# One decoder step on one core: both parts of a head's values in one stationary tile, and four waits of TensorE moved

## The reference

```python
n = rms_norm(x, g_mix)                       # the first norm
q, k, v, hc, bc, cc = split(n @ w_in)        # 16 heads of 64; 1024 conv channels
q, k = rms_norm(q, q_norm), rms_norm(k, k_norm)
attn = dilated_attention(q, k, v, rel_bias)  # softmax(q k / 8 + bias) @ v
conv = bc * short_conv(cc * hc)
h = x + concat[rms_norm(attn), rms_norm(conv)] @ w_out
h = h + (silu(n2 @ w_gate) * (n2 @ w_up)) @ w_down     # n2 = rms_norm(h)
h = h + sigmoid(rms_norm(h) @ w_ple_gate) * (p @ w_ple_proj)
```

## Time and profile before

| | |
|---|---|
| median of 3 runs | 2536.05 us (2533.64 to 2537.11) |
| the profiled execution's own time | 2535.68 us |
| its span, first to last instruction | 2534.1 us |
| PE busy | 2481.5 us, 98% |
| DVE, ACT, POOL busy | 69%, 37%, 10% |
| mean granted clock of TensorE | 0.992 of 2.4 GHz |

### The profile page before, as it was taken

The page is one execution under the profiler, slowest core; times in us unless marked ns, Lnnn a source line. Parts: engine busy times, 40 slices in busy tenths (PEclk is TensorE's granted clock), DMA queues, the critical chain, the costliest instruction groups (busy, mean ns, idle before and its releaser), DMA issues.

```text
span 2534.1 us, 51880 instructions
## 1 busy us (share of the span) xinstructions
PE 2481.5 (98%) x20462; PEld 2467.8 (97%) x20462; DVE 1753.1 (69%) x2194; ACT 933.4 (37%) x1201; POOL 252.9 (10%) x281
## 2 busy tenths in 40 slices
PE   5999999999989999999999999999999999999998
PEld 5999999999989999999999999999999999999998
DVE  5576777777786899898888889888533322356433
ACT  4333333333432444444444444444322222233331
POOL 1111110111111000000000000000000000143000
PEclk8999999999999999999999999999999999999999
DMA  5343333333333423333433333343655443233331
GB/s 187 121 135 116 124 108 110 106 125 109 118 119 114 162 93 137 118 133 117 150 127 138 133 116 133 116 143 129 222 191 180 161 142 118 78 91 103 112 112 67
DMA packets 99741, 324.00 MB, mean 128 GB/s; under 512 B 18258, under 2 KB 18514, under 8 KB 99168
## 3 DMA queue, kind: packets, MB, share of 16 engines
q1 hardware_dynamic: 72144, 250.25, 30.2%
q0 software_dynamic: 26672, 70.69, 8.1%
q10 hardware_dynamic: 864, 2.24, 0.2%
HBM read 286.80 MB, written 40.65 MB: 129 GB/s over the span
## 4 chain that ended last, share of the span: by engine, by line
PE 93%; DVE 3%; DMA 2%; issue 1%; ACT 1%; POOL 0%; ACTq 0%; DVEq 0%; SPq 0%
PE acc L560 18%; PE acc L564 18%; PE acc L562 18%; PE acc L765 11%; PE acc L766 11%; PE acc L764 11%; DMA wraw<-in_w_down 1%; PE aux L571 1%; PE aux L609 1%; PE aux L653 1%; DVE wlo L1252 1%; PE aux L583 0%; PE aux L582 0%; PE aux L581 0%; PE aux L622 0%
## 5 line engine op out<-in xcount | busy, mean ns | idle before, releaser
L1252 DVE TENSOR_TENSOR wlo<-wraw,whi 128x1024 fp32r<-128x1024 f32 (+1 forms) x276 | 333.3, 1208 | 396.2 <-ACT whi L904 395.5
L904 ACT ACTIVATE whi<-wraw 128x1024 fp32r<-128x1024 f32 (+1 forms) x276 | 285.5, 1035 | 705.5 <-PE acc L564 651.7
L764 PE MATMUL acc<-xb_hi,whi 128*128 128x260 f32 x1228 | 347.7, 283 | 4.4 <-DVE xb_lo_t L1643 4.4
L765 PE MATMUL acc<-xa_lo,whi 128*128 128x260 f32 x1228 | 348.4, 284 | 0.0
L766 PE MATMUL acc<-xa_hi,wlo 128*128 128x260 f32 x1228 | 348.3, 284 | 0.0
L766 PE MATMUL acc<-xb_hi,wlo 128*128 128x260 f32 x1228 | 347.4, 283 | 0.0
L764 PE MATMUL acc<-xa_hi,whi 128*128 128x260 f32 x1228 | 346.8, 282 | 0.0
L560 PE MATMUL acc<-slots_a,whi 128*128 128x260 f32 x1536 | 313.3, 285 | 0.0
L564 PE MATMUL acc<-slots_a,wlo 128*128 128x260 f32 x1536 | 309.4, 283 | 0.0
L562 PE MATMUL acc<-slots_a,whi 128*128 128x260 f32 x1536 | 309.4, 283 | 0.0
L560 PE MATMUL acc<-slots_b,whi 128*128 128x260 f32 x1408 | 284.7, 284 | 4.8 <-ACT hid L1194 3.2
(11 more groups left out here) (290 smaller groups left out, 5087.0 us busy)
## 6 DMA issues: line engine op xcount, KB each, us to landing
wraw<-in_w_in SPq DMA_DIRECT2D x96, 512.0 KB, 3.6
blocks<-in_w_gate SPq DMA_DIRECT2D x88, 512.0 KB, 6.0
blocks<-in_w_up SPq DMA_DIRECT2D x88, 512.0 KB, 5.9
wraw<-in_w_down SPq DMA_DIRECT2D x48, 448.0 KB, 3.4
wraw<-in_w_out SPq DMA_DIRECT2D x32, 512.0 KB, 3.5
wraw<-in_w_ple_gate SPq DMA_DIRECT2D x32, 512.0 KB, 3.6
slots_b<-f_dram SPq DMA_DIRECT2D x28, 520.0 KB, 4.6
f_dram<-sig_t POOLq DMA_DIRECT2D x22, 520.0 KB, 3.2
```

Of the source, the lines that this page charges most:

```text
L764: mm(to, w_h, hi, start=p == 0, stop=False)
L765: mm(to, w_h, lo, start=False, stop=False)
L904: on(whi[:, u % HILO, 0:width], wraw[:, u % RAW, 0:width], ACT.Copy).then_inc(s_whi, 1)
L1252: V.tensor_tensor(wlo[:, u % HILO, 0:width], wraw[:, u % RAW, 0:width], whi[:, u % HILO, 0:width].bitcast(F32), ALU.subtract).then_inc(s_w ...
```

## The change

Six edits. **Values:** one tile `v_both` holds, for each head e, the high part in that head's 64 columns and the low part of the same values in the other 64. One pass with the high probabilities and one with the low ones then give the high sums in the head's own 64 rows and the low sums in the other 64. ACT copies the low rows across to `o_low`, DVE adds them. ACT writes the high part in two copies, DVE the low part in two subtractions. **First norm:** the squares come in four groups behind g = 0 to 3, the sum over partitions behind unit 5, its spreading behind unit 6; q too is copied out unscaled, and k, q and v are scaled at g = 6. **x:** the piece 0 goes first on SP, ahead of the first weights; SP takes the even pieces and ACT the odd ones. **Last attention:** it stands behind units 3 to 14 of the conv half, with what follows it (the last operand at i = 13, the attention norm at i = 15). **Down:** the first two units of chunk 0 go to four spare banks. **Hidden tiles** of chunk 1 are loaded one to a unit from m = 5, the last three in chunk 1, which waits for its two parts apart.

```diff
-X_SQUARES = (range(0, 5), range(5, 10), range(10, KT))
+X_SQUARES = (range(0, 4), range(4, 8), range(8, 12), range(12, KT))
...
+    def first_down(m):
+        return (spare, spare_low, acc_of(0), acc_of(1))[m]
...
@@ SP
-                    load_x(1)
-                    load_x(3)
+                    load_x(2)
...
-                    load_x(5)
-                    load_x(7)
+                    load_x(4)
+                    load_x(6)
+        load_x(0)
         pair(FIRST, 0, first=True)
...
+            if m >= 5:
+                load_hidden(1, m - 5)
...
@@ PE
-                    done = products(aux[:, BANK_O, (q0 + skip) * P:(q0 + 2) * P], vhi[:, kb, :], vlo[:, kb, :],
-                                    pthi[:, kb, skip:2, :], ptlo[:, kb, skip:2, :], kb == 0,
-                                    kb == max(q0, 1))
+                    out, values = aux[:, BANK_O, (q0 + skip) * P:(q0 + 2) * P], v_both[:, kb, pair_of // 2, :]
+                    mm(out, values, pthi[:, kb, skip:2, :], start=kb == 0, stop=False)
+                    done = mm(out, values, ptlo[:, kb, skip:2, :], start=False, stop=kb == max(q0, 1))
...
-                if a is None and g == 2:
+                if a is None and g == 5:
                     pe.wait_ge(s_bias, 1)
                     pe.wait_ge(s_xadd, KT - 1)
...
-            if i == 3:
-                pe.wait_ge(s_read, T_CONV + 3)
-            if 2 <= i <= PAIR_UNITS + 1:
-                attention(KA - 1, i - 2, final=True)
+            if 3 <= i <= PAIR_UNITS + 2:
+                attention(KA - 1, i - 3, final=True)
...
+        pe.wait_ge(s_nroot, N_FFN)
         for b in range(4):
-            if b < 2:
-                pe.wait_ge(s_ev, 6 * PAIRS - 2 * (1 - b))
-            if b == 0:
+            if b >= 2:
                 pe.wait_ge(s_cp, 2 * PAIRS)
-            else:
-                pe.wait_ge(s_read, T_D + b - 1)
+                pe.wait_ge(s_ev, 6 * PAIRS)
...
@@ ACT
+            if g in (5, 9):
+                e = (g - 5) // 4
+                act.wait_ge(s_pv, 4 * a + 2 * (e + 1))
+                on(o_low[e * HD:(e + 1) * HD, :], aux[(1 - e) * HD:(2 - e) * HD, BANK_O, :], ACT.Copy).then_inc(s_olow, 1)
...
-        for g in range(0, PIECES, 2):
+        for g in range(1, PIECES, 2):
...
@@ DVE
-                dve.wait_ge(s_pv, 4 * a + 2 * (e + 1))
-                V.tensor_copy(hid[e * HD:(e + 1) * HD, a, 0:SEQ], aux[e * HD:(e + 1) * HD, BANK_O, :]).then_inc(s_o, 1)
+                rows = slice(e * HD, (e + 1) * HD)
+                dve.wait_ge(s_olow, 2 * a + e + 1)
+                V.tensor_tensor(hid[rows, a, 0:SEQ], aux[rows, BANK_O, :], o_low[rows, :], ALU.add).then_inc(s_o, 1)
```

## The result

The changed kernel takes **2514.19 us** (median of 4 runs, 2513.75 to 2514.97) against 2536.08 us before (4 runs beside it): ratio 0.9915, 95% interval 0.9902 to 0.9927. It is faster by 21.9 us, not by 30. The profiled execution took 2514.97 us, with a span of 2513.4.

A forecast was written before the change was run, and what follows sets the result against it. PE, busy 2481.5 of 2534.1 us, was taken to bound the kernel. Terms 14.5 + 10.2 + 2.4 + 3.0 = 30.1 us, taken from 2535.7, gave 2505.6 us; the range was 2495 to 2517.

The forecast's parts named there:

- rival (b): Value products: removed matmuls were not the bound, PE waits for the probabilities instead; 2514 to 2525 us, chance 0.14.
- First norm, 14.5: First turn: earlier PE start and sums without a wait, less a new wait for v's copy; 14.5 us, bounds 12.9 to 19.5.
- fall of the clock: First turn, behind PE's wait for the copy of v: a stretch at half clock, costing 2.0 us.
- Value products, 10.2: Pair loop and last attention: 96 fewer matmuls on PE save 10.2 us, bounds 9.5 and 11.0.
- The 0.5 of the last attention: Value products there: 12 of the removed matmuls, worth 1.4 us, counted as 0.5 because DVE is late.
- The cover of ACT's copy: Value products: two units of PE work hide ACT's copy of low rows, cost nothing; uncovered, 9.6 us.
- Last attention, 2.4: Start of conv half: later attention saves 2.4 us of PE's waiting, half clock stays; bounds 0 and 5.0.
- the wait for unit 1: Start of conv half: PE's unit 3 waits some 4.3 us for DVE's reading of unit 1.
- Start of down, 3.0: Start of down: spare banks and hidden-tile order remove waits and half clock; 3.0 us, bounds 0.5 and 6.1.
- PE's waits for `hid`: Start of down: PE's waits for ACT's copies would remain at 1 to 3 us in all.

The follow-up runs named there:

- experiment 5: Changed kernel with POOL's load of cached values one unit later and DVE's copy of v ahead of four additions of squares: 2502.52 us.
- experiment 7: Kernel before with only the value products changed (two passes instead of three, ACT's copy of the low rows, DVE's addition): 2529.42 us.
- experiment 2: Changed kernel with the last attention back behind units 2 to 13 of the conv half, POOL's queue as before: 2511.11 us.

## Why the prediction held, and where it missed

Sign and range held; the gain was 21.9 us where I had 30.1. The time lies just past the band of my own forecast (2498 to 2514), in the band that I had given to rival (b), but (b) is not why: the removed matmuls paid in the seven turns, and the loss stands in the last attention. That the range held with such a loss in it is owed to its width. By its own steps:

- **First norm, 14.5: right** (14.0), and by its steps: PE's start, the wait for the copy of v with a fall of the clock, sums without a wait. Small misses cancel: the wait was 0.5 us longer, and units 4 and 5 took 54.88 - 41.74 = 13.1 us where two units take 11.7, so that the fall of the clock cost 1.4 and not 2.0. (Two figures of the prediction are a little off: unit 2 of the kernel before ended at 49.39 - 15.03 = 34.4 and not 34.2, and 2505.6 less 2.0 is 2503.6.) How much of the 14.0 the earlier start gives by itself was not tried apart. That the additions ahead of the copy are what PE's wait for v comes from is shown by experiment 5, where only their order changes.
- **Value products, 10.2: mechanism right, size off** (8.5 - 0.6 = 7.9 by experiment 7). The seven turns of the changed kernel give 8.6 / 84 = 0.102 us a matmul; I had read 0.115 off two steps of one timeline. The 0.5 of the last attention was a small loss, by rival (b). The cover of ACT's copy held.
- **Last attention, 2.4: the step that failed.** It came out as a loss, outside its bounds of 0 and 5.0, though the wait for unit 1 came as forecast (4.35 for 4.3). The step followed PE and DVE and did not name POOL, which carries the residual tiles and the load of cached values for this stage in one queue. The one line left behind there cost 2514.2 - 2506.7 = 7.5 us, of which 220.4 - 213.3 = 7.1 in this stretch: 5.6 of waiting and some 2.6 of the 5.3 us at half clock, less 1.2 of new short waits, in sum 7.0 by these rows. With it moved, the stretch wins 3.4, near the 2.9 that I had, but by luck: the shift is worth 4.1 by experiment 2 and not 2.4, and the products lose some 0.6 where I had a gain of 0.5.
- **Start of down, 3.0: size about right, reason wrong.** 1.6 in this profile, 3.1 to 4.2 in the eight others with the new order of the hidden tiles. PE's waits for `hid` came to 3.3, over the 1 to 3 that I had set. I gave most of the term to the spare banks. They only move the waits a few units on, to where ACT's copy stands behind a split that waits for weights. The order earns it: without it the time is 3.1 us up. Which part of the order, the two tiles together or the last three in chunk 1, was not tried apart; the wait of 5.58 stands behind the two together.
- **The clock**: the fall that I set behind the wait for v came, at 0.54. The Trainium skill, "TensorE: Matmul & The Clock Gate", Part 1 (The HAM clock gate), says that idling closes the gate; I had taken it that a short wait may leave it open. The runs have both: 0.59 behind 1.96 us, 1.00 behind 0.68.

## What to carry to other kernels

When a step is moved, list every queue that feeds it, those that only issue loads too, and ask of each entry whether what it waits for has moved with it: a load that waits ahead of its time holds all that stands behind it. Put the copy that frees a PSUM slot ahead of work in the same queue that nobody waits for yet; regrouping that work only moves the wait. A wait removed at a slot is worth nothing while the engine that frees the slot is itself held by weights.

## What was not expected of the hardware

In these profiles a long wait cost more than its length, and a short one nothing beyond it. The 5.64 us at the value product were followed by 5.3 us at 0.50; the 1.35 and 1.24 us at the start of down, close behind one another, by none. Of the waits between, one of 1.79 us at the same place, in the kernel with v copied first, was followed by 0.55 over 3.8 us, though no other wait stood near it. And the 260 KB tile issued at 734.95 behind the 1 MB load landed only for 741.97, some 7 us later, where the median of that load is 3.3 us in the same profile. The two shared POOL's queue, and the small one came last; but a load of weights on SP in the same stretch took 7.9 us too, against a median of 3.5, so whether the queue or the traffic held the tile is not shown.
